# A streaming encoder step on one core: projections, attention and output projection woven into one program with both feed-forward blocks

## The reference, cut to what matters

```python
# layer 0: recurrent mixer, then feed-forward
h = h + mlstm_layer(rmsnorm(h, norm_mix[0]), ...)
h = h + swiglu(rmsnorm(h, norm_ffn[0]), w_gate_up[0], w_down[0])
k_all, v_all = shared_kv(h, g_kv, w_kv, pos)          # one K/V projection, rotary on K, 4 heads of 64
h = h[:, META:]
# layer 1: sliding-window attention, then feed-forward
q = rope(rmsnorm(h, norm_mix[1]) @ b_w_q)              # 16 heads of 64
s = q @ [k_meta, k_window(128)] * scale                # prompt: per chunk of 64 queries
p = softmax([s, sink])                                 # the sink takes part in the sum only
h = h + (p @ [v_meta, v_window]) @ b_w_o
h = h + swiglu(rmsnorm(h, norm_ffn[1]), w_gate_up[1], w_down[1])
y = rmsnorm(h, g_final)
```

## Time and profile before

| what | us |
|---|---|
| median of 3 runs | 2777.96 |
| the profiled execution | 2776.1 |
| its span, first to last instruction | 2774.4 |
| PE busy | 2613.4 (94%) |
| DVE busy | 1090.0 (39%) |
| ACT busy | 635.5 (23%) |
| POOL busy | 605.7 (22%) |

### The profile page before, as it was taken

How to read it: one execution, slowest core, us unless ns; L and a number is a source line. 1 busy time by engine, 2 the same in 40 slices (tenths; PEclk the granted TensorE clock), 3 DMA queues, 4 the chain that set the end, 5 groups by cost and what they waited for, 6 DMA issues and landing times. The chain is left out here.

```text
span 2774.4 us, 37746 instructions
## 1 busy us (share of the span) xinstructions
PE 2613.4 (94%) x15390; PEld 2553.6 (92%) x15390; DVE 1090.0 (39%) x2199; ACT 635.5 (23%) x1390; POOL 605.7 (22%) x503
## 2 busy tenths in 40 slices
PE   8999999989999999999988956598999999999998
PEld 7988899989999999999987945598999999999997
DVE  6444454153333333323365336624433333323334
ACT  5222223141111111111123414403211111111112
POOL 2212222212212221121233530032122212122111
PEclk9999999999999999999999978899999999999999
DMA  4544464101111111111112254421111111111111
GB/s 142 150 124 142 140 172 136 54 24 54 34 43 46 46 39 44 41 46 39 39 48 82 74 128 105 118 79 31 39 46 46 46 39 43 42 46 39 46 39 76
DMA packets 272832, 191.79 MB, mean 69 GB/s; under 512 B 53208, under 2 KB 259820, under 8 KB 272644
## 3 DMA queue, kind: packets, MB, share of 16 engines
q1 hardware_dynamic: 246324, 174.27, 21.6%
q10 hardware_dynamic: 25584, 15.04, 2.1%
q0 software_dynamic: 768, 0.27, 0.1%
HBM read 148.74 MB, written 42.34 MB: 69 GB/s over the span
## 5 line engine op out<-in xcount | busy, mean ns | idle before, releaser
L584 POOL TENSOR_TENSOR wl<-raw,wh 128x512 fp32r<-128x512 f32 x260 | 331.4, 1299 | 1330.7 <-ACT wh L576 1330.7
L706 PE MATMUL psum<-xh,wl 128*128 128x400 f32 (+1 forms) x1872 | 430.0, 338 | 0.0
L706 PE MATMUL psum<-xl,wh 128*128 128x400 f32 (+1 forms) x1872 | 428.3, 337 | 0.0
L706 PE MATMUL psum<-xh,wh 128*128 128x400 f32 (+1 forms) x1872 | 427.2, 336 | 0.0
L848 DVE TENSOR_TENSOR h<-h,psum 128x384 f32<-128x384 f32 (+1 forms) x528 | 264.4, 552 | 285.1 <-PE psum L726 267.4
L706 PEld LDWEIGHTS psum<-xh,wl 128*128 128x128 f32 x1872 | 336.6, 188 | 0.0
L706 PEld LDWEIGHTS psum<-xl,wh 128*128 128x128 f32 x1872 | 336.5, 188 | 0.0
L706 PEld LDWEIGHTS psum<-xh,wh 128*128 128x128 f32 x1872 | 335.8, 188 | 0.0
L1498 PE MATMUL psum<-xh,wh 128*128 128x384 f32 (+1 forms) x792 | 274.8, 347 | 5.3 <-DVE xl L1640 2.5
L1498 PE MATMUL psum<-xl,wh 128*128 128x384 f32 (+1 forms) x792 | 270.6, 342 | 0.0
L1498 PE MATMUL psum<-xh,wl 128*128 128x384 f32 (+1 forms) x792 | 269.3, 340 | 0.0
(11 more groups left out here) (238 smaller groups left out, 3491.0 us busy)
## 6 DMA issues: line engine op xcount, KB each, us to landing
raw<-in_w_gate_up SPq DMA_DIRECT2D x88, 512.0 KB, 3.8
raw<-in_w_down SPq DMA_DIRECT2D x44, 512.0 KB, 3.5
raw<-in_a_w_in SPq DMA_DIRECT2D x24, 512.0 KB, 4.6
fr_qkv<-qkv_d SPq DMA_DIRECT2D x36, 256.0 KB, 4.0
qkv_d<-fr_tmp SPq DMA_DIRECT2D x32, 192.0 KB, 2.0
qr_d<-tmp ACTq DMA_DIRECT2D x8, 584.0 KB, 2.8
x_loaded<-og_d SPq DMA_DIRECT2D x8, 584.0 KB, 5.6
hn_d<-fr_hn_turned SPq DMA_DIRECT2D x36, 128.0 KB, 3.4
```

The source lines that it names most:

```text
L584: pool.tensor_tensor(wl[:, p % 3, v], raw[:, self.raw_of(p), v], wh[:, p % 3, v].bitcast(F32), ALU.subtract).then_inc(self.w_lo, 1)
L706: y = pe.matmul(psum[:, bank + c, 0:nt], w[:, k, :], x[:, k, t0:t0 + nt], start=(k == 0 and m == 0), stop=(k == KD - 1 and m == 2))
```

## The change

`dense`, `Prep`, `Prefetch`, `attention` and the separate `ffn1` go. Their work is done by a class `Mid` inside `front`'s program, between the two `Ffn` blocks, with shared semaphores that count on; only `final` stays a program of its own. No loop is left on the engines.

```diff
+FIRST0, FIRST1, SPREAD1 = 16, 37, 25
+OG_LOAD = {33: 0, 34: 1, 37: 2}
+OG_SPLIT = {34: 0, 35: 1, 40: 2}
...
+        for z in range(2 * NSTEP):
+            slot = FIRST0 + z if z < NSTEP else FIRST1 + ((z - NSTEP) * SPREAD1) // NSTEP
+            self.at_score[slot], self.at_turn[slot + 2], self.at_value[slot + 3] = z, z, z
...
             def _(pe): ...
+            m.tensor(pe)
+            f1.tensor(pe, m.bank_free)
...
-            f.vector(dve)
+            f.vector(dve, m.split_behind)
+            m.vector(dve)
+            f1.vector(dve)
```

In `Mid.scalar` the squares of chunk 2 stand behind `swap(0)`, which waits for `leave(0)` on DVE and by it for the norm of chunk 0. Feed-forward 1 is entered early: chunk 0 is split at slot 76 and chunk 1 at slot 80. In `Ffn.tensor` of both blocks the ones-products move:

```diff
-                if q in (1, 4, 6):
-                    total((q - 1) // 2 if q < 6 else 2)
+        totals_after = (0, 3, 6) if self.early else (3, 5, 7)
...
+                if q in totals_after:
+                    total(totals_after.index(q))
```

More of the change, by code:

```diff
@@ L33 @@
 NMC = SEQ // MCH
[L36 to L52, removed]
+KEPT = META + CHUNK
+KW = META + WINDOW
+SK = KEPT + TS
+NP = SEQ // CHUNK
+NSTEP = NP + 2
+FIRST0, FIRST1, SPREAD1 = 16, 37, 25
+OG_LOAD = {33: 0, 34: 1, 37: 2}
+OG_SPLIT = {34: 0, 35: 1, 40: 2}
+PM, VW, XT, PV, RD, XV = 3072, 3200, 3328, 3456, 3712, 3968
 def build(nc, a, upto=99):
@@ L143, in weight_tile @@
         return b.rearrange("p (k n) -> p k n", k=KD)
[L145 to L171, removed]
@@ L174, in _build @@
[L174 to L220, removed]
@@ L222, in _build @@
[L222 to L235, removed]
@@ L502, in _build @@
-    S = dict(locals())
-    phases = [
-        lambda: run(front, nc, a, S, two(wk, 3)),
-        lambda: run(dense, "kvq", [Group(0, 1, wk, 3, "rope_k"), Group(2, 4, wq, 4, "rope_q"),
-                                   Group(10, 1, wv, 3, "plain_v")], None, prep=True, tables=True),
-        lambda: run(attention, nc, a, S, two(wo1, None)),
-        layer1_out,
-        lambda: run(ffn1),
-        lambda: run(final, nc, a, S),
-    ]
+    S = dict(locals())
+    phases = [lambda: run(front, nc, a, S), lambda: run(final, nc, a, S)]
@@ L516, with __init__ @@
 class Ffn:
-    def __init__(self, nc, a, s, name, layer, gain, pre, parity, tok):
-        self.s, self.tok, self.gain, self.pre, self.parity = s, tok, gain, pre, parity
+    def __init__(self, nc, a, s, name, layer, gain, parity, base, early, tok, before=None):
+        self.s, self.tok, self.gain, self.parity, self.base, self.early = s, tok, gain, parity, base, early
         at, sem = s["at"], s["sem"]
@@ L846, in down_out @@
                 t0, nt = tok[c]
-                dve.wait_ge(self.dn_done, 24 * i + q + 1)
+                dve.wait_ge(self.dn_done, self.z["dn_done"] + 24 * i + q + 1)
                 dve.tensor_tensor(h[:, m, t0:t0 + nt], h[:, m, t0:t0 + nt], psum[:, (q + 3) % 6, 0:nt], ALU.add)\
                     .then_inc(self.dn_evac, 1)
-        x_low(0)
-        x_low(1)
-        sums(0)
-        x_low(2)
+                if after is not None and i == self.passes - 1:
+                    after(dve, q)
+        for c in range(3):
+            if c == 2 or not self.early:
+                for k in range(KD):
+                    self.x_low(dve, c, k)
+                if c and not self.early:
+                    self.sums(dve, c - 1)
         recip(0)
@@ L859, in vector @@
             take(self.gate, 1, c, (3 * c + 2) % 6, 3 * c + 3)
+            if c == 0 and not self.early:
+                self.sums(dve, 2)
             if c < 2:
-                sums(c + 1)
                 recip(c + 1)
@@ L882, in front @@
+def front(nc, a, s):
     at, sem, psum, ident, ones, h = s["at"], s["sem"], s["psum"], s["ident"], s["ones"], s["h"]
@@ L1187, in _ @@
             f.sync(sp)
-            sp.wait_ge(f.w_lo, 2 * f.n_weights)
-            for u in range(2):
-                nx.load(sp, u)
             sp.wait_ge(meta_st, 16)
@@ L1448, in _ @@
             f.gpsimd(pool)
-            for u in range(2):
-                nx.scale(pool, u)
-                pool.wait_ge(f.gu_done if u == 0 else f.dn_done, (12 if u == 0 else 24) * f.passes)
-                nx.split(pool, u)
+            m.gpsimd(pool)
+            f1.gpsimd(pool)
         @block.tensor
```

1641 lines of the change are left out of this document (916 added, 725 removed).

## The result

The changed kernel takes 2672.5 us (median of 4 runs, 2671.9 to 2673.4) against 2777.8 us before (median of 4 as well): a ratio of 0.9623, 95% interval 0.9606 to 0.9639. The profiled execution has a span of 2671.6 us at a mean granted clock of 0.991 (before: 2774.4 us, 0.977). The forecast was 2657.0 us, 15.5 us too low.

A forecast was written before the change was run, and what follows sets the result against it. TensorE's work and its waits between the feed-forwards set the end. Middle: 255 dense + 94 attention + 17.5 entry + 5 small waits = 371.5 against 478.8 us; 2776.1 - 107 - 8.5 - 5 = 2655.6, median 2657, range 2628 to 2698.

The forecast's parts named there:

- third rival: Joints of the middle: sums locked against VectorE, or read-backs late by 11 us, plus clock; 10 to 15 us more, 2670; chance 0.12.
- Feed-forward 0's ones-products: Moved behind groups 3, 5, 7 from 1, 4, 6, taking away the wait for sums: 5 us less, between 0 and 7.
- Feed-forward 1's entry: Input split two chunks ahead of the first matmul; of 10.5 us lost some 2 stay: 8.5 us less.
- The entry to the projections: Start of the middle: waits of 3 and 7 us for GpSimd's sums, ones-products and a clock fall; 17.5 us.
- first rival: More is won: GpSimd's sums at 1.08 us are found done, entry costs 5 us, small waits vanish; 2640; chance 0.12.
- Attention on TensorE: Prompt and sample steps, turning caches and output rows, and going back to dense groups in the middle: together 94 us.
- Small waits: Four slots turning output rows, 3 us, and the change of weights and banks at slot 36, 2 us: 5 us.
- Do the other engines keep up?: Attention slots: ScalarE 5.3 and VectorE 4.3 of TensorE's 6.7 us, later 4.0 and 3.6 of 4.6; it fits.
- sign of 8: Slots 16 to 33 over 8 us apart would mean every attention slot waits: 1 us each, 2700; chance 0.14.
- Transfers: Read-backs of pair 1 and the attention result, covered by 17 and 14 us: 0 us, 11 if cover is short.
- a wait of over 3 us at slot 36 or 37: Sign in the profile after, on TensorE in the middle, that would mean the third rival.
- Slower: In-order queues make each middle slot one chain with nothing run ahead: 230 us more, 2890; chance 0.04.

The follow-up runs named there:

- experiment 2: Changed kernel with SyncE's read-back of pair 1's K, V and Q issued in slots 34, 35, 37 instead of 33, 34, 35: 2659.3 us.
- experiment 7: Kernel of experiment 2 with turned probabilities one slot behind the scores instead of two, values two instead of three: 2794.8 us.
- Experiments 3 and 4: Each on the changed kernel: third ones-product behind projection group 5 instead of 3, 2673.3 us; chunk 2's squares ahead of the first swap, 2673.0 us.
- experiment 6: Kernel of experiment 2 plus early chunk 2 squares, weight scaling ahead of low parts, norm tables in VectorE's gaps and chunk 2's root earlier: 2652.2 us.
- experiment 9: Kernel of experiment 6 with pair 1's 18 attention steps in 18 consecutive output slots instead of 25: 2650.2 us.
- experiment 8: Kernel of experiment 7 with a step's sum and reciprocal ahead of maxima, copy and rotation on VectorE: 2680.5 us.

## Why the prediction was right or wrong

The sign, the order of size and the mechanism were right: 2672.5 us lies within the range, and at the upper end of the forecast's own 2642 to 2675. The largest term by which it was too low is 13.5 us of late read-backs, one half of the third rival; its other half, sums locked against VectorE, did not come. Without them the kernel of experiment 2 took 2659.3 us, 2 us from the forecast, but that closeness is in part luck: attention 8 us dearer than counted is offset in part by the entry and feed-forward 0, which gave 2.7 and 1.9 us more than counted. No run undoes the weaving itself: that it makes the gain rests on the profiles before and after, and experiment 7 varies only the distance of the steps' parts. Nor was it tried what the rounding of weights, now on ScalarE, is worth alone.

- *Feed-forward 0's ones-products: 5 us.* Measured 6.9 between the two profiles and 4.7 by undoing it. The last matmul of feed-forward 0 starts between 1422.1 and 1424.9 us in the kernels here that have the same instructions up to there, so the profiles alone could not tell 5 from 7.
- *Feed-forward 1's entry: 8.5 us.* 8.4 between the profiles; undoing the early split costs 4.9. So the step's size came out right, but only part of it belongs to the early split; that the rest comes from the output projection now ending chunk by chunk is my reading, not tested.
- *The entry to the projections: 17.5 us*, with waits of 3 and 7 us. Measured waits 1.0, 2.2 and 7.8 us, the ones-products about 1.8 and the slow matmuls behind the long wait 14 times 0.144, 2.0: 14.8 us. GpSimd's sums took 1.12 us (median of 21) and not 1.35. That is close to the 1.08 of the first rival, but TensorE found the third sum no earlier for it, as the prediction's argument against that rival had it. The description held; what it did not see is that the wait was replaceable. Experiments 3 and 4 took it away without any gain, because the chain of norm, rotation and weights behind it ended no earlier.
- *Attention on TensorE: 94 us.* What is left of the 377.6 us of experiment 2 after 256.1 of dense matmuls (254.2, and 1.9 because the 288 of 400 columns come 0.183 us apart), 14.8 of entry and 4.7 of waits is 102 us, and the same by the same sum in experiment 6. The step itself was right, 2.35 us from its first product to the next dense matmul. Part of the missing 8 us is the change from a dense group into small products, which I counted at nothing: 0.1 us more than a matmul's spacing, in every slot. The rest is not resolved.
- *Small waits: 5 us.* 4.7 in the kernel of experiment 2, 2.8 in the changed one, where some are hidden by the late read-backs.
- *Do the other engines keep up?* Yes, as worked out; experiment 9 is the sharper test of it. Slots 16 to 33 are 6.7 to 7.6 us apart but for the first three, which are shorter, a little more than the 6.5 to 7 of the prediction and below its sign of 8.
- *Transfers: "I count 0, and 11 us if the cover is short."* **This is the step that failed**: the cover was short, and the late read-backs cost 13.5 us. The sign that was named for it, "a wait of over 3 us at slot 36 or 37", came elsewhere: the waits of 3.78 and 6.56 us stand at slots 38 and 41, in attention, and the first chunk, the only one of the result that the prediction timed, was not late; chunks 1 and 2 were. The failure is in how I looked. I set the time from request to need (14 and 17 us) against the longest wait of before, and never walked SyncE's queue, where 5 and 9 issues of pair 1's read-back at 0.4 to 2.6 us each stood ahead of the two requests for the result. And I compared with the slot in which TensorE wants the data, where the splitting instructions stand up to five slots ahead of it and block two in-order queues that carry the attention steps.

The sum: 371.5 - 2.7 (entry) - 0.3 (small waits) + 13.5 (read-backs) + 8 (attention) + 1.1 (400 columns) = 391.1 against 391.1 measured; it closes because the 8 us are a remainder.

*Slower, 0.04.* The mechanism of that rival ("the in-order queues make each slot one chain") is real, and experiment 7 is one slot away from it: 2794.8 us, slower than the kernel before. The argument against it in the prediction, that scores, turns and products stand two and three slots apart, is what holds it off with this order of VectorE's queue; with the reciprocal moved ahead one slot is enough (experiment 8, 2680.5 us). 0.04 was fair for this kernel, but with the order as it is the margin is one constant.

## What to carry to other kernels

When work is laid between dense groups, what decides is not the load of the engines but what stands ahead of the short instruction that TensorE needs. Walk each in-order queue, the DMA-issuing one too, to the instruction that blocks first, not to the one that needs the data: here the place of a sum and a reciprocal of 0.33 us together was worth 114 us, and the order of a few DMA issues 13. And a wait that is named in the profile is worth its length only if the chain behind it has slack; twice a wait of 7.8 us was removed and came back up to five groups later, as 1.7 and 6.3 us and as 7.5 us, until the third link (4.4 us) and the fourth (2.3 us) were taken out too.

## What the runs showed of the hardware

- A wait of TensorE is dearer than its length. Single waits of 3.8, 6.6 and 7.8 us were each followed by some 14 matmuls at half clock (1.2 instead of 2.4 GHz), about 2 us more each time, and some 30 waits of 2.6 us in a row held the granted clock at 0.79 to 0.89.
- An issue on SyncE is not of one size: 18 stores of 192 KB took 0.34 us in the median and up to 0.84 (0.50 and 0.71 between the read-backs), and of the first four 192 KB reads of Q, 4.25 us together, three took about 0.5 us and one 2.56. From 1645 to 1700 us, where the DMA engines were busy 0.57 of the time, the issuing queue itself was the place of the delay. That the busy engines make an issue longer was not tested.
- VectorE's products with two SBUF inputs took 1.05 and 1.34 us beside GpSimd's sums, and 0.56 when GpSimd was idle:

```profile
1450.30 1.05 DVE L1230 TENSOR_TENSOR mid_cos<-mid_cos,rstd 128x384 f32<-128x384 f32 x1
1451.27 1.34 DVE L1230 TENSOR_TENSOR mid_sin<-mid_sin,rstd 128x384 f32<-128x384 f32 x1
...
1462.37 0.56 DVE L1230 TENSOR_TENSOR mid_cos<-mid_cos,rstd 128x384 f32<-128x384 f32 x1
1462.85 0.55 DVE L1230 TENSOR_TENSOR mid_sin<-mid_sin,rstd 128x384 f32<-128x384 f32 x1
```

The Trainium skill (SBUF — State Buffer, "two separate sides") has such products and a GpSimd operation that reads SBUF take turns whole: whichever starts first keeps the shared port pair until it ends. The rows agree for VectorE: a product of 0.56 us that first waits for the rest of a sum of 1.1 comes to anything up to 1.7. They do not show the cost on GpSimd that the prediction weighed: its sums stayed between 0.99 and 1.21 us.
